# Norm weights multiplied beside the sums of squares, and a feed-forward fed by unscaled rows

## What is computed

```python
def rms_norm_2(x, g):
    xf = x.astype(jnp.float32)
    y = xf * lax.rsqrt(jnp.mean(xf * xf, axis=-1, keepdims=True) + RMS_EPS)
    return (y * g.astype(jnp.float32)).astype(x.dtype)

def swiglu(h, w_gate, w_up, w_down):
    return (jax.nn.silu(h @ w_gate) * (h @ w_up)) @ w_down

def second_block(x, ...):
    h = rms_norm_2(x, g_pre_mix)
    m = chunk_relpos_attention(h, w_qkv, w_o, rel_bias)   # 16 heads, causal by chunks
    x = x + rms_norm_2(m, g_post_mix)
    h = rms_norm_2(x, g_pre_ffn)
    x = x + rms_norm_2(swiglu(h, w_gate, w_up, w_down), g_post_ffn)
    return x
```

## Time and profile before

| | |
|---|---|
| time, median of 3 runs | 864.47 us (862.73 to 865.64) |
| profiled execution | 864.02 us |
| its span, first to last instruction | 862.0 us |
| PE busy | 777.6 us (90%) |
| DVE busy | 413.3 us (48%) |
| ACT busy | 331.4 us (38%) |
| POOL busy | 24.4 us (3%) |
| mean granted TensorE clock | 0.957 |

### The profile page before, as it was taken

One profiled execution on the slowest core, in us unless ns is written; L12 is line 12 of the kernel. 1 busy time (PEld: TensorE's weight loads), 2 busy tenths in 40 slices (PEclk: granted clock), 3 DMA queues, 4 the chain that ended last, 5 costly groups with the idle time before them and its releaser, 6 DMA issues.

```text
span 862.0 us, 12683 instructions
## 1 busy us (share of the span) xinstructions
PE 777.6 (90%) x5320; PEld 633.2 (73%) x5320; DVE 413.3 (48%) x714; ACT 331.4 (38%) x581; POOL 24.4 (3%) x49
## 2 busy tenths in 40 slices
PE   8999899999989799966876588999997999999995
PEld 8788688888767675543444348897666999999994
DVE  5747746777656611100110037466666554455443
ACT  5556464555434211110110025454555444444442
POOL 1100000000000000000000004000001000000000
PEclk9999999999999889988987989999998999999998
DMA  9626285544976779999999997743221556555301
GB/s 340 205 99 195 74 286 205 167 160 162 365 249 265 292 327 422 420 421 420 420 422 421 420 396 283 291 146 101 98 98 50 191 161 200 182 195 179 115 1 49
DMA packets 77402, 204.57 MB, mean 237 GB/s; under 512 B 6945, under 2 KB 35233, under 8 KB 64801
## 3 DMA queue, kind: packets, MB, share of 16 engines
q1 hardware_dynamic: 77344, 203.75, 63.1%
HBM read 202.69 MB, written 1.05 MB: 236 GB/s over the span
## 4 chain that ended last, share of the span: by engine, by line
PE 67%; DMA 15%; DVE 7%; ACT 4%; issue 3%; SPq 2%; POOL 1%; ACTq 0%; DVEq 0%; POOLq 0%
PE ps L553 50%; PE ps L831 4%; DMA ext<-in_w_gate_e 3%; DMA big<-in_w_up_e 3%; DMA raw<-in_w_up_e 3%; DMA ext<-in_w_up_e 3%; SPq L434 2%; DMA gb<-in_gate_b 2%; PE ps L810 2%; PE ps L852 2%; DVE wl L1375 2%; PE ps L910 2%; PE ps L733 1%; PE ps L611 1%; ACT junk L1032 1%
## 5 line engine op out<-in xcount | busy, mean ns | idle before, releaser
L1375 DVE TENSOR_TENSOR wl<-raw,wh 128x1024 fp32r<-128x1024 f32 (+3 forms) x180 | 213.9, 1200 | 161.0 <-ACT wh L1023 160.7
L1023 ACT CAST wh<-raw 128x1024 fp32r<-128x1024 f32 (+3 forms) x180 | 183.7, 1031 | 123.1 <-PE ps L553 122.9
L553 PE MATMUL ps<-fra,wh 128*128 128x256 f32 x1168 | 216.2, 287 | 6.6 <-DVE fra L1405 2.8
L553 PEld LDWEIGHTS ps<-fra,wh 128*128 128x128 f32 x1168 | 186.2, 195 | 9.4 <-DVE fra L1405 3.5
L553 PE MATMUL ps<-wh,fra 128*128 128x512 f32 (+2 forms) x604 | 185.9, 389 | 5.4 <-DVE gb L1600 2.3
L553 PE MATMUL ps<-fra,wl 128*128 128x256 f32 x584 | 167.2, 286 | 0.0
L553 PEld LDWEIGHTS ps<-wh,fra 128*128 128x128 f32 x604 | 110.4, 188 | 29.2 <-issue 3.4
L553 PE MATMUL ps<-wl,fra 128*128 128x512 f32 (+2 forms) x302 | 115.7, 383 | 0.0
L553 PEld LDWEIGHTS ps<-fra,wl 128*128 128x128 f32 x584 | 114.1, 195 | 0.0
L553 PE MATMUL ps<-wh,frb 128*128 128x512 f32 x240 | 74.5, 391 | 0.0
L831 PE MATMUL ps<-ext,big 128*32 128x256 f32 x528 | 59.3, 442 | 13.3 <-DMA raw<-in_w_up_e 6.2
(11 more groups left out here) (225 smaller groups left out, 793.7 us busy)
## 6 DMA issues: line engine op xcount, KB each, us to landing
ext<-in_w_up_e SPq DMA_DIRECT2D x18, 1024.0 KB, 26.2
raw<-in_w_in SPq DMA_DIRECT2D x16, 1024.0 KB, 5.1
ext<-in_w_gate_e SPq DMA_DIRECT2D x15, 1024.0 KB, 26.0
raw<-in_w_down_e SPq DMA_DIRECT2D x14, 1024.0 KB, 22.5
ext<-in_w_down_e SPq DMA_DIRECT2D x13, 1024.0 KB, 26.4
raw<-in_w_qkv SPq DMA_DIRECT2D x12, 1024.0 KB, 14.0
raw<-in_w_gate_e SPq DMA_DIRECT2D x11, 1024.0 KB, 27.3
raw<-in_w_gate SPq DMA_DIRECT2D x11, 1024.0 KB, 5.1
```

What stands on the lines that cost most here:

```text
L553: t = e.matmul(o, a, w, start=first and n == 0, stop=final and n == 2, skip_group_check=not check)
L1023: e.copy(halves(q)[0], piece_view(q)).then_inc(*up("wh", q))
L1375: e.tensor_tensor(l, piece_view(q), h.bitcast(F), ALU.subtract).then_inc(*up("wl", q))
```

## The change

It does five things. (1) In the attention start, the spread of the key factor moves from between the queries and the keys to behind the first piece of the values, and DVE's `diag`, `krow` and key multiplications move with it. (2) `add_normed` is cut in two: DVE multiplies each PSUM bank by the norm weight as soon as ACT has squared it, and later one instruction multiplies by the row factor and adds `X`, in halves of 512 columns. ACT squares with a scale of 1/32, so that the running sum is a mean, and POOL needs two instructions instead of three; row 0's factor waits for its own two squares only. (3) The rows that are transposed for the feed-forward are `X` itself, without the norm factor, in three groups of tiles (0 to 3, 4 and 5, 6 and 7), each as soon as its column half is added; a tile of 256 columns has half a bank (`FFN_AT`), and the high and low halves and the first gate product wait tile by tile. The useless products go from 18 to 9. (4) The factor is found later; PE spreads it behind the first up product into bank 2, and DVE multiplies each gate product by it before Silu (`scaled_gate`), which ACT then does in place. The up product is left without the factor, and the last norm takes it up: its epsilon becomes epsilon times the mean plus epsilon of the row (`eps of out`). (5) The last sums are added and stored in four parts of 256 KB.

```diff
-WARM = (24, 16, 12, 18)
+WARM = (24, 16, 12, 9)
+FFN_AT = ((0, 0), (1, 0), (2, 0), (3, 0), (6, 0), (7, 0), (0, 1), (1, 1))
...
         for i in range(2):
-            e.wait_ge(*at("added", "out", i))
-            load("out", ov[:, i, :], X[:, i, :])
-        e.wait_ge(s_load["out"], 32)
+            for c in range(2):
+                cols = slice(512 * c, 512 * c + 512)
+                e.wait_ge(*at("added", "out", i, c))
+                load("out", ov[:, i, cols], X[:, i, cols])
+        e.wait_ge(s_load["out"], 64)
...
+                    if row:
+                        e.wait_ge(*at(*row, p.k0 + kk))
...
+        def spread(name, b):
+
+            enter(b, name, 0)
+            e.wait_ge(*at("diag", name))
+            for i in range(2):
+                t = e.matmul(bank[b][:, P * i:P * i + P], ones, diag[:, P * i:P * i + P], start=True, stop=True)
+            t.then_inc(*up("spread", name))
+
         whole(qk(0, 0))
-        enter(6, "krow")
-        e.wait_ge(*at("diag"))
-        for i in range(2):
-            t = e.matmul(bank[6][:, P * i:P * i + P], ones, diag[:, P * i:P * i + P], start=True, stop=True)
-        t.then_inc(*up("krow turned"))
         whole(qk(2, 1))
-        whole(vals(0, 0))
+        first_vals = vals(0, 0)
+        next(first_vals)
+        spread("krow", 6)
+        whole(first_vals)
...
-        turn("ffn", H, 8, (4, 5, 6, 7), [[at("scaled", "ffn", i)] for i in range(2)])
+        for tiles in ((0, 1, 2, 3), (4, 5), (6, 7)):
+            for k in tiles:
+                enter(FFN_AT[k][0], "lo", "ffn", k)
+            for i in range(2):
+                e.wait_ge(*at("added", "o", i, tiles[0] // 4))
+                for k in tiles:
+                    t = e.transpose(ffn_rows(k)[:, P * i:P * i + P], X[:, i, P * k:P * k + P], ident)
+            t.then_inc(*up("turn", "ffn", tiles[0]))
...
                 whole(features(("fu", c), 5 + 2 * (c % 2), hT, ("a", c)))
+                if c == 0:
+                    spread("ffn row", 2)
...
-            square(rms("ffn")[0][:, i:i + 1], X[:, i, :], junk, "ffn", i)
+                square(rms("o")[0][:, 2 * c + i:2 * c + i + 1], bank[2 * c + i][:, :], junk, "o", c, i, scale=1 / 32)
+        for k in range(8):
+            e.wait_ge(*at("turn", "ffn", (0, 4, 6)[(k >= 4) + (k >= 6)]))
+            e.activation(hT[0][:, k, :], ffn_rows(k), ACT.Copy, scale=G[:, G_FFN2 + k:G_FFN2 + k + 1]).then_inc(
+                *up("hi", "ffn", k))
         split_to(q_o + AHEAD)
-        high("ffn", hT[0], 8, (4, 5, 6, 7), G_FFN2)
+        for i in range(2):
+            e.wait_ge(*(at("squared", "o", 1, 1) if i == 0 else own()))
+            square(rms("ffn")[0][:, i:i + 1], X[:, i, :], junk, "ffn", i, scale=1 / 32)
...
-                e.activation(S[0], bank[4 + 2 * z][:, :], ACT.Silu).then_inc(*up("silu", c, 0))
-                whole(stream(("fu", c)))
+                e.wait_ge(*at("scaled gate", c, 0))
+                e.activation(S[0], S[0], ACT.Silu).then_inc(*up("silu", c, 0))
...
             for i in range(2):
+                for c in range(2):
+                    e.wait_ge(*at("squared", name, c, i))
+                    e.tensor_tensor(H[:, i, 512 * c:512 * c + 512], bank[2 * c + i][:, :],
+                                    gb[:, row, 512 * c:512 * c + 512], ALU.mult).then_inc(*up("gained " + name, i, c))
+            for i in range(2):
+                e.wait_ge(*at("gained " + name, i, 1))
                 e.wait_ge(*at("factor", name, i))
                 for c in range(2):
-                    t = e.scalar_tensor_tensor(H[:, i, 512 * c:512 * c + 512], bank[2 * c + i][:, :],
-                                               rms(name)[1][:, i:i + 1], gb[:, row, 512 * c:512 * c + 512], ALU.mult, ALU.mult)
-                    t.then_inc(*up("normed " + name, i, c))
-                e.wait_ge(*own())
-                e.tensor_tensor(X[:, i, :], X[:, i, :], H[:, i, :], ALU.add).then_inc(*up("added", name, i))
+                    xs = X[:, i, 512 * c:512 * c + 512]
+                    e.scalar_tensor_tensor(xs, H[:, i, 512 * c:512 * c + 512], rms(name)[1][:, i:i + 1], xs, ALU.mult,
+                                           ALU.add).then_inc(*up("added", name, i, c))
...
+        def scaled_gate(c):
+            if c:
+                e.wait_ge(*at("al", c - 1))
+            e.wait_ge(*at("piece", last["fg", c]))
+            e.tensor_tensor(S[0].rearrange("p (j n) -> p j n", j=2),
+                            bank[4 + 2 * (c % 2)][:, :].rearrange("p (j n) -> p j n", j=2),
+                            krow.unsqueeze(1).to_broadcast([P, 2, 256]), ALU.mult).then_inc(*up("scaled gate", c, 0))
...
+                if c == 0:
+                    e.wait_ge(*at("factor", "ffn", 1))
+                    spread("ffn row", rms("ffn")[1])
+                    spread_row("ffn row", 2)
+                    scaled_gate(c)
```

More of the change, by code:

```diff
@@ L578, in tokens, with features @@
                 yield
-        def features(key, b0, y, freed, ready=(), later=()):
+        def features(key, b0, y, freed, ready=(), later=(), row=None):
             yh, yl = y
@@ L972, in tensor @@
             if c < 11:
-                whole(features(("fg", c), 4 + 2 * (c % 2), hT, ("silu", c), [at("lo", "ffn", 0, 1)] if c == 0 else (),
-                               [at("lo", "ffn", 4, 1)] if c == 0 else ()))
+                whole(features(("fg", c), 4 + 2 * (c % 2), hT, ("scaled gate", c), row=("lo", "ffn") if c == 0 else None))
                 whole(features(("fu", c), 5 + 2 * (c % 2), hT, ("a", c)))
+                if c == 0:
+                    spread("ffn row", 2)
             if c:
@@ L1029, in stream, with square @@
                 yield
-        def square(acc, part, scratch, *point):
-            e.activation(scratch[:, 0:part.shape[-1]], part, ACT.Square, accum_out=acc).then_inc(*up("squared", *point))
+        def square(acc, part, scratch, *point, scale=1.0):
+            e.activation(scratch[:, 0:part.shape[-1]], part, ACT.Square, scale=scale, accum_out=acc).then_inc(
+                *up("squared", *point))
         def keep(dst, b, key, *point):
@@ L1351, in scalar @@
                 e.wait_ge(*(at("squared", "ffn", 1) if (i, c) == (0, 0) else own()))
-                square(rms("out")[0][:, 2 * c + i:2 * c + i + 1], bank[2 * c + i][:, :], junk, "out", c, i)
+                square(rms("out")[0][:, 2 * c + i:2 * c + i + 1], bank[2 * c + i][:, :], junk, "out", c, i, scale=1 / 32)
     def general_scalar(e):
@@ L1810, in vector, with spread, spread_row, keep_k @@
         low_rows(4)
-        def qk(c, d):
-            yield from stream(("qkv", c))
-            for j in range(2 if c > 1 else 0):
+        def spread(name, factors):
+            for i in range(2):
+                t = e.tensor_scalar(diag[:, P * i:P * i + P], ident, factors[:, i:i + 1], None, ALU.mult)
+            t.then_inc(*up("diag", name))
+        def spread_row(name, b):
+            e.wait_ge(*at("spread", name))
+            e.tensor_copy(krow, bank[b][:, 0:256]).then_inc(*up(name, 0))
+            e.wait_ge(*own())
+        def keep_k(c, d):
+            for j in range(2):
                 e.wait_ge(*at("piece", last["qkv", c]))
-                if (c, j) == (2, 0):
-                    e.wait_ge(*at("krow"))
                 e.tensor_tensor(kT[:, 4 * c + 2 * j - 8:4 * c + 2 * j - 6, :],
@@ L1853, in vector @@
         whole(first)
+        whole(stream(("qkv", 2)))
         e.wait_ge(*at("factors"))
[L1855 to L1863, removed]
+        spread("krow", rr)
+        vals = stream(("qkv", 4))
+        next(vals)
+        spread_row("krow", 6)
+        keep_k(2, 1)
+        whole(vals)
         fill = second_half()
@@ L1976, in gpsimd, with root_of_means @@
         e.memset(bias[0:64, :, 192:256], NEG).then_inc(*up("bias masked"))
+        def root_of_means(name, i, eps):
+            ss, r = rms(name)
+            e.wait_ge(*at("squared", name, 1, i))
+            e.tensor_scalar(ss[:, i:i + 1], ss[:, i:i + 1], ss[:, i + 2:i + 3], eps, ALU.add, ALU.add).then_inc(
+                *up("mean", name, i))
+            e.wait_ge(*own())
+            e.tensor_tensor(r[:, i:i + 1], ss[:, i:i + 1], half[:, 0:1], ALU.pow).then_inc(*up("factor", name, i))
         for i in range(2):
[L1978 to L1979 removed]
+            root_of_means("o", i, EPS)
+        ss, r = rms("ffn")
         for i in range(2):
             e.wait_ge(*at("squared", "ffn", i))
[L1982 removed]
+            e.tensor_scalar(ss[:, i:i + 1], ss[:, i:i + 1], EPS, None, ALU.add).then_inc(*up("mean", "ffn", i))
+            e.wait_ge(*own())
+            e.tensor_tensor(r[:, i:i + 1], ss[:, i:i + 1], half[:, 0:1], ALU.pow).then_inc(*up("factor", "ffn", i))
+        e.tensor_scalar(ss[:, 2:4], ss[:, 0:2], EPS, None, ALU.mult).then_inc(*up("eps of out"))
+        e.wait_ge(*own())
         for i in range(2):
[L1984 to L1985 removed]
+            root_of_means("out", i, ss[:, 2 + i:3 + i])
```

40 lines of the change are left out of this document (19 added, 21 removed).

## The result

The changed kernel takes 850.88 us (median of 4 runs, 850.12 to 853.15) against 865.06 us before (4 runs, 862.73 to 865.78); the ratio is 0.9845, 95% interval 0.9818 to 0.9872. Timed again beside the experiments the ratio was 0.9862 (0.9847 to 0.9878). The time lies in the range of 850.6 to 857.2, 0.3 us above its lower end and 2.5 us under the forecast of 853.4.

What follows compares the result with a forecast made beforehand. PE is busy throughout the feed-forward's 132 us, so gains come only from starting earlier or ending sooner. Terms -1.8 - 6.9 + 0.6 + 0 - 3.0 = -11.1 us give 853.4 us, range 850.6 to 857.2.

Steps and rivals of the forecast that it cites:

- Key factor: Attention start: PE's wait for the diagonal ahead of the key factor's spread goes, the spread itself stays; -1.8 us.
- Projection to gate product: Output projection to first gate product: gate product starts at 658.3 instead of 665.16; -6.9 us.
- lock of DVE against POOL: At both norms: POOL's second power begins ahead of DVE's first addition, so 0; if behind it, 0 to +0.9 us.
- Spread of the row factor: Behind the first up product: PE waits 0 to 0.3 us and spreads for 0.44; +0.6 us.
- Loop: Feed-forward's 11 chunks: one more DVE instruction of 0.69 us ahead of Silu in each; cost 0.
- End: Last norm and stores: additions done at 856.5 instead of 858.97, span ends at 858.9 instead of 862.0; -3.0 us.
- the first rival: Hole before the gate product: clock still falls, 3.4 us at half rate lose 1.7; 855.1 us, chance 0.36.
- rivals of the stores: End: four transfers' starts and ends come one after the other, +5.3 us; 858.7 us, chance 0.05.
- the tiles: Transposes before the gate product: tiles 6 and 7 wait for all low halves, +2 us; 855.4 us, chance 0.04.
- the loop: Feed-forward chunks: scaled gate puts weight rests behind PE's need; 865.5 us at 1.1 us late per chunk, chance 0.03.

Runs made afterwards that it cites:

- second profile of the changed kernel: The changed kernel run and profiled once more with no edit, beside the experiments: 852.09 us, ratio 0.9862 against the kernel before.
- first profile: The changed kernel's original profiled execution, with the whole change against the kernel before: 851.18 us, span 849.3.
- one pause filled: Kernel before with five useless products in PE's 1.4 us pause ahead of the second attention's first scores: 864.62 us, ratio 1.001.

## Why the prediction was right

Step by step, against the second profile of the changed kernel, in which the clock does not fall:

- Key factor: forecast -1.8, measured -2.0. The wait went and nothing came in its place.
- Projection to gate product: forecast -6.9, measured -7.0 (13.47 to 6.51). Inside it, the halves of the addition came every 0.66 us (four in 2.73, each 0.74 long), not 0.6, and the low halves of tiles 0 and 1 were the last wait, as said. The lock of DVE against POOL cost nothing, as forecast, but it was not seen at all in this order: in the first profile the second power (648.26 to 648.82) began 0.16 us ahead of the first addition and took 0.56, and that addition took as long as the three behind it. A lock that goes to whichever starts first would have held it. What the rows show is the other order, in the kernel before, where the power began 0.2 us behind an addition and took 1.44.
- Spread of the row factor: forecast +0.6, measured +0.7 (187.02 to 187.73), of which the spread itself takes 0.44 (665.98 to 666.42).
- Loop: forecast 0; PE lacks 0.06 us in 180, and six more scalings in each chunk cost waits at the start alone.
- End: forecast -3.0, measured -2.9. The parts of 256 KB moved in about 0.7 us each, not 0.6, and the end came 2.5 us behind the last addition, not 2.4.

The sum of these is -11.2 against the forecast -11.1. The experiments take apart only some of it: the key factor whole, 2.0 of the 7.0 us up to the gate product and 1.7 of the 2.9 at the end (the weights multiplied beside the squares), and 0.5 of the end (four stores). That the rest comes from unscaled rows, tiles and halves is read from the waits, and no run takes one of these back by itself.

The step that failed is the sum's assumption that the stretch between, the attention, stays as it was: it took 1.5 us less than in the profile of before, because the clock did not fall behind the pause ahead of the first scores. I had read the clock only at the places that the change touches. With it the measured distance from the first query product on is 12.7 us. The medians lie 14.2 us apart, 11.1 to 15.7 by the interval, which holds 11.1 as well as 12.7: the times alone do not tell them apart.

That the time lies in the range is in part luck. At 850.88 us it is just under the 851 to 856 that the prediction gives for the forecast alone. And in the profiled execution the first rival came, whose time is 855.1; that it took 851.18 is for the most part the attention's 1.5 us and 1.6 us of the stage ahead, neither of which is in the sum.

The first rival was half right. In the first profile the clock did fall, for 3.4 us and 1.4 us of cost; in the second it did not. Its price (1.7) was near, and its place right. The rule of the Trainium skill (TensorE: Matmul & The Clock Gate, Part 4: PE-mode transpose) that the full clock does not engage for transposes was not borne out here: the clock came back at 664.8 in the kernel before, when PE had done only transposes since the useless products, and it stayed at 1.00 through all 16 in the second profile. Why it fell among them in the first and not in the second, with the same waits, is open. The rivals of the stores, the tiles and the loop did not come.

## What to carry to other kernels

Work that a norm puts between two products can be taken off the path by linearity: multiply by the weights beside the squares, feed the next product unscaled, and give the factor to a later and smaller tile. Each such step was worth the time between the two waits that bound it, and here that could be read off the trace to 0.2 us. Read the granted clock behind every pause of PE downstream, not only at the edit: with work moved by 2 us, a fall of the clock 26 us later was gone, worth 1.5 us here. So judge an edit by the lengths between fixed instructions and not by the total alone.

## What the runs showed that I had not expected

- With one pause filled the attention gained 1.4 us and the feed-forward lost 1.9, with no change in sum (ratio 1.001): the fall in the old hole lasted 10.2 us instead of 6.8. Whether the filling caused that is open.
- The same pause of 1.4 us was followed by a fall of the clock in the one profile of the kernel before, and by none in nine profiles with the work ahead of it shortened by 2 us.
- The stage ahead of the second block, the same code in all, took 516.1 to 519.3 us in twelve profiles, as much as most single edits here are worth.
